# A fused decoder-layer kernel whose opening is written out with four raw and three normalised tile buffers

## What is computed

```python
def rmsnorm(x, g):
    xf = x.astype(jnp.float32)
    y = xf * lax.rsqrt(jnp.mean(xf * xf, axis=-1, keepdims=True) + EPS) * g.astype(jnp.float32)
    return y.astype(x.dtype)

def layer_forward(x, attention, rnn_conv_buf, rnn_h0, ffn_buf, lp):
    hn = rmsnorm(x, lp['norm_mix'])
    q, k, v, f_logit, xr, gr = jnp.split(hn @ lp['w_in'], SPLIT_IDX, axis=-1)
    ... attention over q, k, v; recurrent branch over xr, gr
    x = x + merged @ lp['w_out']
    ... x = x + gated convolution FFN of rmsnorm(x)
```

## Times and profile before

| what | us |
|---|---|
| three timed runs | 3356.98, 3363.10, 3363.46 |
| their median | 3363.1 |
| the profiled execution | 3355.78 |
| its span, first to last instruction | 3353.6 |
| start of the first eviction of the opening | 18.89 |
| end of the last eviction of the opening | 105.06 |
| first projection product | 111.40 |

### The profile page before, as it was taken

One profiled execution on the slowest core, in us unless ns is written; L12 is line 12 of the kernel. 1 busy time (PEld: TensorE's weight loads), 2 busy tenths in 40 slices (PEclk: granted clock), 3 DMA queues, 4 the chain that ended last, 5 costly groups with the idle time before them and its releaser, 6 DMA issues.

```text
span 3353.6 us, 46822 instructions
## 1 busy us (share of the span) xinstructions
PE 3037.8 (91%) x15400; PEld 2659.0 (79%) x15400; DVE 1447.2 (43%) x1910; ACT 757.9 (23%) x1529; POOL 1212.9 (36%) x575
## 2 busy tenths in 40 slices
PE   4798998957788888897899999999999998999998
PEld 4798987843354545455898999999999998999998
DVE  4212433348566555534415445555445554222221
ACT  5100332212232333333202000000000002434343
POOL 1011111133566565633766222222222222455443
PEclk7899999967799898998899999999999999999999
DMA  5211343355787677754345111111111114555553
GB/s 182 94 65 55 90 104 94 86 106 160 237 250 231 182 228 236 229 174 136 113 132 154 44 47 51 51 42 48 45 42 51 51 38 155 183 182 188 180 194 110
DMA packets 253580, 422.52 MB, mean 126 GB/s; under 512 B 49265, under 2 KB 156954, under 8 KB 248906
## 3 DMA queue, kind: packets, MB, share of 16 engines
q1 hardware_dynamic: 167986, 322.58, 30.8%
q10 hardware_dynamic: 85152, 97.07, 9.6%
q0 software_dynamic: 288, 1.05, 0.1%
HBM read 337.21 MB, written 83.46 MB: 125 GB/s over the span
## 4 chain that ended last, share of the span: by engine, by line
PE 69%; DMA 7%; POOL 7%; DVE 6%; issue 5%; SPq 4%; ACT 2%; ACTq 0%; POOLq 0%; DVEq 0%
PE PS L2452 33%; PE PS L2154 13%; PE PS L2534 4%; PE PS L2536 4%; PE PS L2535 4%; POOL prod L905 3%; DMA Kpg<-in_cache_k 2%; PE PS L2346 2%; SPq L581 2%; PE PS L2443 1%; SPq L574 1%; DMA xin<-in_x_prompt 1%; PE PS L2135 1%; DVE YT L2097 1%; DMA mixT<-RX 1%
## 5 line engine op out<-in xcount | busy, mean ns | idle before, releaser
L2452 PE MATMUL PS<-MH,VS 128*128 128x416 f32 x4000 | 1086.9, 352 | 11.2 <-POOL VS L968 9.0
L2452 PEld LDWEIGHTS PS<-MH,VS 128*128 128x128 f32 x4000 | 750.1, 188 | 23.2 <-issue 12.3
L2452 PE MATMUL PS<-ML,VS 128*128 128x416 f32 x2000 | 701.4, 351 | 0.0
L962 POOL TENSOR_TENSOR VR<-VR,gains 128x1024 f32<-128x1024 f32 x52 | 98.7, 1898 | 791.6 <-PE PS L2452 694.9
L2452 PEld LDWEIGHTS PS<-ML,VS 128*128 128x128 f32 x2000 | 376.7, 188 | 4.2 <-issue 0.8
L1025 POOL TENSOR_TENSOR DL<-DR,DH 128x1408 fp32r<-128x1408 f32 x80 | 258.6, 3233 | 286.1 <-ACT DH L1446 286.0
L905 POOL TENSOR_TENSOR prod<-Kpg,qb 128x1024 f32<-128x1024 f32 x118 | 284.0, 2407 | 174.0 <-DMA Kpg<-in_cache_k 137.9
L2346 PE MATMUL PS<-PT,VA 128*65 128x416 f32 (+16 forms) x816 | 340.0, 501 | 4.0 <-ACT PT L1307 3.5
L2534 PE MATMUL PS<-GH,DH 128*128 128x416 f32 x880 | 314.3, 357 | 16.2 <-DVE GL L2079 8.6
L2154 PE MATMUL PS<-XH,WH 128*128 128x416 f32 x840 | 307.2, 366 | 19.8 <-issue 11.6
L2536 PE MATMUL PS<-GH,DL 128*128 128x416 f32 x880 | 310.5, 353 | 0.0
(11 more groups left out here) (273 smaller groups left out, 4501.7 us busy)
## 6 DMA issues: line engine op xcount, KB each, us to landing
Kpg<-in_cache_k SPq DMA_DIRECT2D x256, 256.0 KB, 4.2
Vpg<-in_cache_v SPq DMA_DIRECT2D x256, 256.0 KB, 4.1
DR<-in_w_down SPq DMA_DIRECT2D x80, 704.0 KB, 4.1
gT<-GO ACTq DMA_DIRECT2D x110, 208.0 KB, 1.9
VR<-in_w_up SPq DMA_DIRECT2D x44, 512.0 KB, 3.5
GRb<-gT SPq DMA_DIRECT2D x31, 416.0 KB, 5.1
WR<-in_w_stream SPq DMA_DIRECT2D x21, 512.0 KB, 3.6
GRa<-gT SPq DMA_DIRECT2D x24, 416.0 KB, 5.8
```

Source lines behind the costliest of these rows:

```text
L2452: mm = e.matmul(PS[:, j, 0:BW], w[:, u, k], x[:, k, cols(j)], start=(k == 0 and q == 0), stop=(k == KC - 1 and q == 2))
```

## The change

`xin` and its statistics `st0` have four slots, `hn` has three; `xst` and the PSUM banks stay at two. The loops of the opening are written out on all engines. The order changes thus:

- SyncE issues four tiles' loads at the start; the load of tile t waits for the turning of tile t-4. The loads of the first two blocks of `w_in` are issued after tiles 4 and 5 in place of ahead of the loop.
- ScalarE squares tiles 0, 1 and 2 before it empties tile 0, and then empties t and squares t+3. In `empty` the copy to `XH` comes ahead of the copy to `xst`; the store of `xst` now waits for both.
- VectorE normalises t+2 and then makes `XL` of t, where it was t+1. `low` now waits for the first of the two copies.
- TensorE transposes the normalised rows of a tile before the raw ones. It still gives one count at the end of the sixteen.
- GpSimd clears the last slot after tile 12 is turned, not after tile 14.

```diff
-        xin = sb("xin", [P, 2, DM], F32, m0)
-        hn = sb("hn", [P, 2, DM], F32, m0)
+        xin = sb("xin", [P, NXI, DM], F32, m0)
+        hn = sb("hn", [P, NHN, DM], F32, m0)
...
-            for u in range(2):
-                e.dma_start(WR[:, u], a["w_stream"][u]).then_inc(w_ld[u], 16)
-            with e.Fori(0, 7) as i:
-                for v in range(2):
-                    e.wait_ge(x_tp, 2 * i + v + 1)
-                    e.dma_start(xin[:, v], a["x_prompt"][0][bass.ds((2 * i + 2 + v) * P - NMETA, P), :])\
-                        .then_inc(x_ld[v], 16)
+            for t in range(1, NXI):
+                e.dma_start(xin[:, t], a["x_prompt"][0][t * P - NMETA:(t + 1) * P - NMETA, :]).then_inc(x_ld[t], 16)
+            for t in range(NXI, NT - 1):
+                e.wait_ge(x_tp, t - NXI + 1)
+                e.dma_start(xin[:, t % NXI], a["x_prompt"][0][t * P - NMETA:(t + 1) * P - NMETA, :])\
+                    .then_inc(x_ld[t % NXI], 16)
+                if t - NXI < 2:
+                    u = t - NXI
+                    e.dma_start(WR[:, u], a["w_stream"][u]).then_inc(w_ld[u], 16)
...
-            e.wait_ge(x_tp, 15)
+            e.wait_ge(x_tp, NT - NXI)
             e.memset(xin[0:TAIL, 0], 0.0).then_inc(x_pad, 1)
...
-                e.activation(xst[:, u, :, 0:rows], raw[:, :, 0:rows], ACT.Copy).then_inc(x_ev, 1)
-                e.activation(XH[:, :, bass.ds(t * P, rows)], nrm[:, :, 0:rows], ACT.Copy).then_inc(x_ev, 1)
-                e.wait_ge(x_ev, 2 * t + 1)
+                e.activation(XH[:, :, t * P:t * P + rows], nrm[:, :, 0:rows], ACT.Copy).then_inc(x_ev, 1)
+                e.activation(xst[:, u, :, 0:rows], raw[:, :, 0:rows], ACT.Copy).then_inc(x_ev, 1)
+                e.wait_ge(x_ev, 2 * t + 2)
...
-            mean_square(0, 0, 16)
-            mean_square(1, 1, 16)
-            empty(0, 0, 0)
-            with e.Fori(0, 7) as i:
-                for v in range(2):
-                    e.wait_ge(x_hn, 2 * i + v + 1)
-                    mean_square(2 * i + 2 + v, v, 16 * i + 32)
-                    empty(2 * i + 1 + v, 1 - v, 16 * (i + v))
+            for t in range(3):
+                mean_square(t)
+            for t in range(NT):
+                empty(t, P if t < NT - 1 else TAIL)
+                if t + 3 == NT - 1:
+                    e.wait_ge(x_last, 16)
+                if t + 3 < NT:
+                    mean_square(t + 3, P if t + 3 < NT - 1 else TAIL)
...
-                e.wait_ge(x_ev, 2 * t + 2)
+                e.wait_ge(x_ev, 2 * t + 1)
...
-            normalise(0, 0)
-            normalise(1, 1)
-            low(0, 0)
-            with e.Fori(0, 7) as i:
-                for v in range(2):
-                    normalise(2 * i + 2 + v, v)
-                    low(2 * i + 1 + v, 1 - v)
+            normalise(0)
+            normalise(1)
+            for t in range(NT):
+                if t + 2 < NT:
+                    normalise(t + 2, P if t + 2 < NT - 1 else TAIL)
+                low(t, P if t < NT - 1 else TAIL)
...
-                for src, b in ((xin, 4 * u), (hn, 4 * u + 2)):
+                for src, b in ((hn[0:rows, t % NHN], 4 * u + 2), (xin[0:rows, t % NXI], 4 * u)):
```

More of the change, by code:

```diff
@@ L34 @@
 NMETA = 16
+NXI = 4
+NHN = 3
 SEQ = 2048
@@ L262, in build @@
         gmix = sb("gmix", [P, DM], F32, m0)
-        st0 = sb("st0", [P, 2, 4], F32, m0)
+        st0 = sb("st0", [P, NXI, 4], F32, m0)
         m0.close()
@@ L385, in build @@
         x_first = sem("x_first")
-        x_ld = [sem("x_ld0"), sem("x_ld1")]
+        x_ld = [sem(f"x_ld{n}") for n in range(NXI)]
         x_pad = sem("x_pad")
@@ L502, in build @@
         gg_lo = sem("gg_lo")
-        yx_ld = [sem("yx_ld0"), sem("yx_ld1")]
+        yx_ld = x_ld[2:4]
+        yx0 = 16 * (NT // NXI)
         y_ev = sem("y_ev")
@@ L522, in _ @@
             e.dma_start(xin[NMETA:P, 0], a["x_prompt"][0][0:P - NMETA, :]).then_inc(x_ld[0], 16)
-            e.dma_start(xin[:, 1], a["x_prompt"][0][P - NMETA:2 * P - NMETA, :]).then_inc(x_ld[1], 16)
-            for u in range(2):
-                e.dma_start(WR[:, u], a["w_stream"][u]).then_inc(w_ld[u], 16)
-            with e.Fori(0, 7) as i:
-                for v in range(2):
-                    e.wait_ge(x_tp, 2 * i + v + 1)
-                    e.dma_start(xin[:, v], a["x_prompt"][0][bass.ds((2 * i + 2 + v) * P - NMETA, P), :])\
-                        .then_inc(x_ld[v], 16)
+            for t in range(1, NXI):
[7 more added lines that the diff above has]
+                    e.dma_start(WR[:, u], a["w_stream"][u]).then_inc(w_ld[u], 16)
             e.wait_ge(x_pad, 1)
@@ L1045, in _, with mean_square, empty @@
             act0 = Steps(e, a0)
-            def mean_square(t, u, n, rows=P):
-                e.wait_ge(x_ld[u], n)
-                act0.inc(e.activation(sqj[0:rows], xin[0:rows, u], ACT.Square, accum_out=st0[0:rows, u, 0:1]))
+            def mean_square(t, rows=P):
+                s = t % NXI
+                e.wait_ge(x_ld[s], 16 * (t // NXI) + 16)
+                if t >= NXI:
+                    e.wait_ge(x_hn, t - NXI + 1)
+                act0.inc(e.activation(sqj[0:rows], xin[0:rows, s], ACT.Square, accum_out=st0[0:rows, s, 0:1]))
                 act0.settle()
-                e.activation(st0[0:rows, u, 1:2], st0[0:rows, u, 0:1], ACT.Sqrt, bias=epsT[0:rows],
+                e.activation(st0[0:rows, s, 1:2], st0[0:rows, s, 0:1], ACT.Sqrt, bias=epsT[0:rows],
                              scale=1.0 / DM).then_inc(x_sq, 1)
-            def empty(t, u, st, rows=P):
+            def empty(t, rows=P):
+                u = t % 2
                 e.wait_ge(x_tp, t + 1)
-                e.wait_ge(x_st[u], st + 1)
+                e.wait_ge(x_st[u], 16 * (t // 2) + 1)
                 raw = PS[:, 4 * u:4 * u + 2, :].rearrange("p a (k n) -> p (a k) n", n=P)
                 nrm = PS[:, 4 * u + 2:4 * u + 4, :].rearrange("p a (k n) -> p (a k) n", n=P)
+                e.activation(XH[:, :, t * P:t * P + rows], nrm[:, :, 0:rows], ACT.Copy).then_inc(x_ev, 1)
                 e.activation(xst[:, u, :, 0:rows], raw[:, :, 0:rows], ACT.Copy).then_inc(x_ev, 1)
-                e.activation(XH[:, :, bass.ds(t * P, rows)], nrm[:, :, 0:rows], ACT.Copy).then_inc(x_ev, 1)
-                e.wait_ge(x_ev, 2 * t + 1)
-                e.dma_start(xT.rearrange("(k p) n -> p k n", p=P)[:, :, bass.ds(t * P, rows)],
+                e.wait_ge(x_ev, 2 * t + 2)
+                e.dma_start(xT.rearrange("(k p) n -> p k n", p=P)[:, :, t * P:t * P + rows],
                             xst[:, u, :, 0:rows]).then_inc(x_st[u], 16)
@@ L1066, in _ @@
             e.wait_ge(x_first, 16)
-            mean_square(0, 0, 16)
-            mean_square(1, 1, 16)
-            empty(0, 0, 0)
-            with e.Fori(0, 7) as i:
-                act0.start(i, 2)
-                for v in range(2):
-                    e.wait_ge(x_hn, 2 * i + v + 1)
-                    mean_square(2 * i + 2 + v, v, 16 * i + 32)
-                    empty(2 * i + 1 + v, 1 - v, 16 * (i + v))
[L1076 to L1081, removed]
+            for t in range(3):
[6 more added lines that the diff above has]
+                    mean_square(t + 3, P if t + 3 < NT - 1 else TAIL)
             e.wait_ge(c_pool, 14)
@@ L1532, in _, with normalise, low @@
             e.wait_ge(c_ld, 16 * 5)
-            def normalise(t, u, rows=P):
+            def normalise(t, rows=P):
+                s = t % NXI
                 e.wait_ge(x_sq, t + 1)
-                if not (isinstance(t, int) and t < 2):
-                    e.wait_ge(x_tp, t - 1)
-                e.reciprocal(st0[0:rows, u, 2:3], st0[0:rows, u, 1:2]).then_inc(d0, 1)
+                if t >= NHN:
+                    e.wait_ge(x_tp, t - NHN + 1)
+                e.reciprocal(st0[0:rows, s, 2:3], st0[0:rows, s, 1:2]).then_inc(d0, 1)
                 e.wait_ge(d0, t + 1)
-                e.scalar_tensor_tensor(out=hn[0:rows, u], in0=xin[0:rows, u], scalar=st0[0:rows, u, 2:3],
+                e.scalar_tensor_tensor(out=hn[0:rows, t % NHN], in0=xin[0:rows, s], scalar=st0[0:rows, s, 2:3],
                                        in1=gmix[0:rows], op0=ALU.mult, op1=ALU.mult).then_inc(x_hn, 1)
-            def low(t, u, rows=P):
-                e.wait_ge(x_ev, 2 * t + 2)
+            def low(t, rows=P):
+                u = t % 2
+                e.wait_ge(x_ev, 2 * t + 1)
                 nrm = PS[:, 4 * u + 2:4 * u + 4, :].rearrange("p a (k n) -> p (a k) n", n=P)
-                c = bass.ds(t * P, rows)
+                c = slice(t * P, t * P + rows)
                 e.tensor_tensor(XL[:, :, c], nrm[:, :, 0:rows], XH[:, :, c].bitcast(F32),
                                 ALU.subtract).then_inc(x_lo, 1)
-            normalise(0, 0)
-            normalise(1, 1)
-            low(0, 0)
-            with e.Fori(0, 7) as i:
-                for v in range(2):
-                    normalise(2 * i + 2 + v, v)
-                    low(2 * i + 1 + v, 1 - v)
```

(18 more changed lines are left out.)

## The result

| | before | changed |
|---|---|---|
| median of 7 runs, us | 3363.46 | 3336.78 |
| lowest and highest | 3356.98 to 3378.87 | 3330.40 to 3350.81 |
| profiled execution, and its span | 3355.78, 3353.6 | 3330.40, 3328.4 |
| first copy out of PSUM in the opening | 18.89 | 17.09 |
| table load (`rh`) issued | 105.25 | 81.97 |

The ratio is 0.9921, with a 95% interval of 0.9896 to 0.9946: 26.7 us less, with some 8 us of uncertainty either way. Forecast were 3333 and a gain of 27. In the two traces the opening is 111.40 - 88.32 = 23.1 us shorter, not 27, and the span 25.2. The other 2.1 came later. The projections' last products start at 691.5 before and 669.9 after (21.6 apart), the first of the output product and FFN at 1657.1 and 1632.6 (24.5), those of the down product at 2809.2 and 2782.7 (26.5).

A forecast was written before the change was run, and what follows sets the result against it. The opening was taken as bound by a ring of latencies, 5.49 us a tile, then by ScalarE at 3.77. Gain 28.3 less 1.0 gave 27 us; from the mean 3359.8 this made 3333, range 3324 to 3346.

The forecast's parts named there:

- The bound: Opening: ScalarE's own work is the dearest of four parts of the new ring, 3.77 us a tile against 5.49 before.
- the load leaving the chain: Opening's tile loads: 7.1 us left for what took 4.1, at most 5.2, so no load is waited for.
- The start: First hn free of GpSimd's WL, 1.54 us sooner; first copy out of PSUM at 17.35 in place of 18.89.
- The cost of the new order of the copies: ScalarE in the opening: the store now waits for the second copy, costing 0.58 us a tile on the path.
- The stores: Two xst slots: a store may take 5.5 us; 3.6 in the median, 6.6 at most before; taken as covered.
- the rival of the stores: Opening: stores end last; at 6.6 us each the period is 4.3, gain 19, time 3341; chance 0.15.
- The second pair of weight blocks: Weight blocks from the third on, issued after the tail's load: said to be sooner too, within the not-kept rival (3360), chance 0.03.
- GpSimd against VectorE: Tiles 2 to 5, when WR lands: shared-port exclusion costs between nothing and 2.1 us; 1.0 taken off the gain.
- VectorE and TensorE's loop: Opening: 6.8 us for two tiles, 3.4 a tile, hidden below 3.77 with 0.7 to spare per two tiles.
- The turning order worth nothing: TensorE turning normalised rows first in the opening gains nothing, since one count is given after all sixteen transposes.
- The sum: Table load issued at 76.9 in place of 105.25, gain 28.3, less 1.0 for GpSimd: 27 us.

The follow-up runs named there:

- 13: Three raw tile slots (xin) in place of four, otherwise the changed kernel: first projection product at 88.8 us, against 88.3 and 87.1 in the changed kernel's two traces.
- 8: Changed kernel with a third xst slot, and xst copied first with its store beside the copy to XH: first projection product at 76.8 us against 88.3.
- 2: Changed kernel with a third xst slot: first projection product at 83.2 us against 88.3, no store waited for.
- 11: The changed kernel run once more without edit: first projection product at 87.1 us against 88.3, waits for stores 4.4 us.
- 14: Two normalised tile slots (hn) in place of three, otherwise the changed kernel: first projection product at 86.7 us against 88.3 and 87.1.
- 1: Changed kernel with the first two weight blocks loaded behind the last tile: first projection product at 86.5 us against 88.3, waits for stores 2.5 us.
- 10: Changed kernel with xst copied first, its store beside the XH copy, and half of each tile's columns loaded from tile 4: first product at 79.5 us.
- 7: Changed kernel with TensorE turning the raw rows first again: first projection product at 86.4 us against 88.3.

## Where the prediction was right and where not

- **The bound, and the load leaving the chain**: right. Squares come 3.80 us apart where 3.77 was reckoned, and no turning and no load is waited for in the middle. The start was right too: the first `hn` took 1.28, and the first copy came at 17.09 for 17.35. 13 shows that the load does come back with a slot less.
- **The cost of the new order of the copies**: right in kind, the 0.50 of idle before each squares row, and in size: with the stores out of the way 8 against 2 gives 3.80 - 3.18 = 0.62 a tile, against 0.58.
- **The stores**: this step failed. "I take the median's side: covered" rested on 3.6 us, the median at 5.49 us a tile. The rows had the warning, the 6.6 at most. At the new pace the median was 4.8 and the first store took 9.76, beside four tiles' and two weight blocks' loads. It cost 4.05 us at tile 2, 0.59 at tile 14 and 0.92 at tile 16 (the last of these the sum had in part). It is the rival of the stores, only not in every tile but mostly where the weight blocks meet them; 11 and 14 also waited at tile 8 (0.74 and 0.56), where there are none, so at two slots the margin is thin throughout. 1, 2 and 10 show it from three sides.
- **The second pair of weight blocks**: left out of the sum. SyncE issues it at 66.7 right behind the tail's load, and of the last stores one takes 6.27. That the one causes the other is read from their order in time; no run moves this pair alone. I had said of these blocks only that they are sooner too.
- **GpSimd against VectorE**: 1.0 was taken, and nothing of it ended up on the path. One hn took 1.90, while ScalarE was idle for the store. In run 2 ScalarE had no such idle time and two hn took 1.91 and 2.53, yet the copies stayed some 3.8 apart but for one at 3.98. In the rows of before one reading was wrong: the second hn (1.87 at 15.17) stood not beside WL, which had ended at 13.98, but beside the second block's WH (2.03 from 13.93). In the changed trace XL, with one SBUF input, ran its 1.22 beside a GpSimd copy, and hn, with two, took as long as if it had waited for WL: WL ended at 25.90, and 1.28 more is 27.2, against 26.97 measured. The Trainium skill ("SBUF — State Buffer", "Who interferes with whom") says that a VectorE instruction with two SBUF inputs contends with a GpSimd one that reads SBUF, and one with at most one such input doesn't; the rows fit.
- **VectorE and TensorE's loop**: right that it hides; its 3.4 was for the lower clock. In 8 a tile took 3.18, below that: a tile's turning at 41.62 took 1.94 at the higher clock (granted in full from 41.5 to 44), against 3.68 at the lower, and the mean over that stretch was 0.85 of full. The 0.7 us to spare per two tiles were too many all the same: by the prediction's own 3.68 for TensorE alone, more than the loop's 3.4, only 2 x (3.77 - 3.68) = 0.2 are left at the lower clock.
- **The turning order worth nothing**: 7 missed its half us by 1.4, but lies within 0.3 of 14, which keeps the order of the change; not contradicted, and not settled below 1 us.
- **The sum**: forecast 27.3, measured 23.1 in the opening. Start +0.3, GpSimd +1.0; against that the table's load was issued at 81.97, not at 76.9, which with the start makes 5.3 lost, nearly all of it the waits for stores (4.64 at tiles 2 and 14, and what tile 16 waited beyond the sum's 0.6), and 0.2 more from there to the first product: 27.3 + 0.3 + 1.0 - 5.3 - 0.2 = 23.1. That the timed medians differ by 26.7 is in part luck: the two traces differ by 2.1 in stages that the change doesn't touch.

## What to carry to other kernels

When a ring of waits is opened by more slots, count every ring that goes through the same stage, the stores' too, and price the next one not at the durations of before but at those of the new pace: a transfer slows as the traffic beside it grows. Slots pay where the ring is tightest; here a third store slot, which the change did not have, paid 4 to 5 us, and the fourth raw and the third normalised slot hardly anything. Two instructions in another order can move a DMA's issue from beside a copy to behind it, and on the engine that sets the pace this costs its full time at every tile, here 0.62 us.

## What the runs showed that I had not expected

The DMA share is not the distance to a limit: it read 0.98 at 283 GB/s, 1.01 at 334 and 1.05 at 326, and I had scaled 0.62 at 191 to a limit of 308. The time to landing of the same 512 KB store went from a median of 3.6 us (two tiles in 11 us) to 4.8 (3.8 us a tile; 4.3 in its second run) and 6.3 (3.2 us a tile), while the loads' median was 4.1, 4.2 and 5.2. And code that doesn't change took from 580.1 to 586.4 us between the first and last projection product in different executions, so gains of a few us have to be read where they arise.
